# A new order for the opening: w_ada transposed, two tiles projected block by block

## What is computed

```python
c_act = jax.nn.silu(c)
mod = c_act @ w_ada[layer] + b_ada[layer]              # 1024 -> 6 * 1024
shift1, scale1, gate1, shift2, scale2, gate2 = split(mod, 6)
h = rmsnorm(x, norm1_gain[layer]) * (1.0 + scale1) + shift1
proj = h @ w_in[layer]                                 # 1024 -> 1280: q 512 | k, v 256 | p 512
```

## Time and profile before

| | us |
|---|---|
| median of 3 runs | 954.5 (954.21 to 955.22) |
| span of the profiled execution | 952.9 |
| what lies around the span, median less span | 1.6 |
| TensorE busy | 927.6 (97%) |
| VectorE busy | 792.6 (83%) |
| ScalarE busy | 512.9 (54%) |

### The profile page before, as it was taken

How to read it: one execution, slowest core, us unless ns; L and a number is a source line. 1 busy time by engine, 2 the same in 40 slices (tenths; PEclk the granted TensorE clock), 3 DMA queues, 4 the chain that set the end, 5 groups by cost and what they waited for, 6 DMA issues and landing times.

```text
span 952.9 us, 14120 instructions
## 1 busy us (share of the span) xinstructions
PE 927.6 (97%) x4404; PEld 770.8 (81%) x4404; DVE 792.6 (83%) x1205; ACT 512.9 (54%) x980; POOL 276.6 (29%) x243
## 2 busy tenths in 40 slices
PE   4999999999999999999999999999999999999998
PEld 4887888878887777888888888888888888888886
DVE  7979999998689879797787977878798787977797
ACT  3247556676444747456464655546456464655543
POOL 0025554451100100704215070330705215070334
PEclk9999999999999999999999999999999999999999
DMA  9978453348255594655555555745655655555624
GB/s 355 399 236 285 159 197 117 109 156 279 96 155 173 176 340 150 245 206 213 209 187 221 176 185 211 263 140 184 224 215 206 211 191 215 177 188 208 220 88 177
DMA packets 96136, 193.97 MB, mean 204 GB/s; under 512 B 6513, under 2 KB 57441, under 8 KB 96097
## 3 DMA queue, kind: packets, MB, share of 16 engines
q1 hardware_dynamic: 90720, 182.02, 54.2%
q10 hardware_dynamic: 5376, 11.47, 3.5%
HBM read 176.30 MB, written 17.17 MB: 203 GB/s over the span
## 4 chain that ended last, share of the span: by engine, by line
PE 87%; DVE 5%; DMA 4%; ACT 2%; issue 1%; SPq 1%; POOL 0%; ACTq 0%; DVEq 0%; POOLq 0%
PE ps L2117 27%; PE ps L2119 27%; PE ps L2118 27%; DMA bs<-bs_scratch 2%; PE ps L2337 2%; DMA raw_u<-in_w_up 1%; PE ps L2216 1%; DVE acc L1360 1%; PE ps L2363 1%; PE ps L2227 1%; DMA ada_in_raw<-in_w_ada 1%; PE ps L2290 0%; DMA bs_scratch<-stg 0%; DMA m_raw<-mixed_scratch 0%; ACT qbd L832 0%
## 5 line engine op out<-in xcount | busy, mean ns | idle before, releaser
L1283 POOL TENSOR_TENSOR x<-x,p1s 128x512 f32<-128x512 f32 x80 | 116.0, 1470 | 422.0 <-ACT p1s L980 421.3
L2117 PE MATMUL ps<-bs,ring 128*128 128x512 f32 x344 | 134.4, 391 | 1.5 <-DVE h_lo L1724 0.7
L2119 PE MATMUL ps<-bs,ring 128*128 128x512 f32 x344 | 133.9, 389 | 0.0
L2118 PE MATMUL ps<-bs,ring 128*128 128x512 f32 x344 | 133.9, 389 | 0.0
L1731 DVE TENSOR_TENSOR ring<-s,ring 128x512 fp32r<-128x512 f32 x88 | 69.8, 811 | 50.3 <-ACT ring L901 50.2
L2117 PE MATMUL ps<-h_hi,ring 128*128 128x512 f32 x272 | 106.1, 390 | 0.5 <-DVE h_lo L1724 0.5
L2118 PE MATMUL ps<-h_lo,ring 128*128 128x512 f32 x272 | 105.8, 389 | 0.0
L2119 PE MATMUL ps<-h_hi,ring 128*128 128x512 f32 x272 | 105.8, 389 | 0.0
L901 ACT ACTIVATE ring<-s 128x512 fp32r<-128x512 f32 x88 | 53.8, 623 | 66.5 <-PE ps L2119 66.5
L2117 PEld LDWEIGHTS ps<-bs,ring 128*128 128x128 f32 x344 | 64.6, 188 | 16.9 <-DMA bs<-bs_scratch 1.9
L2119 PEld LDWEIGHTS ps<-bs,ring 128*128 128x128 f32 x344 | 64.6, 188 | 13.5
(11 more groups left out here) (291 smaller groups left out, 2333.9 us busy)
## 6 DMA issues: line engine op xcount, KB each, us to landing
bs<-bs_scratch SPq DMA_DIRECT2D x166, 512.0 KB, 6.2
stage<-in_w_ada SPq DMA_DIRECT2D x24, 512.0 KB, 5.9
raw_g<-in_w_gate SPq DMA_DIRECT2D x11, 1024.0 KB, 5.2
raw_u<-in_w_up SPq DMA_DIRECT2D x11, 1024.0 KB, 7.4
raw_d<-in_w_down SPq DMA_DIRECT2D x20, 512.0 KB, 4.1
ada_in_raw<-in_w_ada SPq DMA_DIRECT2D x16, 512.0 KB, 12.4
wi_raw<-in_w_in SPq DMA_DIRECT2D x8, 640.0 KB, 15.3
wo_raw<-in_w_out SPq DMA_DIRECT2D x8, 512.0 KB, 5.7
```

The lines of the kernel that those rows point to most:

```text
L1283: pool.tensor_tensor(x1_half(t, 1), x1_half(t, 1), p1s[j][:, :], ALU.add).then_inc(pool_evac, 1)
L2117: pe.matmul(dst, s_hi, m_hi, start=start, stop=False, skip_group_check=onto)
L2118: pe.matmul(dst, s_hi, m_lo, start=False, stop=False, skip_group_check=onto)
L2119: return pe.matmul(dst, s_lo, m_hi, start=False, stop=stop, skip_group_check=onto)
```

## The change

w_ada is also given transposed by the host. A piece is then 128 outputs by all 1024 inputs, and one multiply with c spread over the partitions (`crow`), with an accumulator output, gives the 128 finished sums as a column (`column_sum`). No reduction on TensorE is left for scale1, shift1, scale2 and shift2; gate1 keeps its own. x tiles 0 and 1 are scaled, split and projected block by block. SP loads w_ada pieces and W_in rows in turns, the shift pieces behind all W_in rows. The shift product comes behind both tiles, only two parts of tile 1 after it. The small vectors, the bias table's store and the constants' loads move between the blocks. `sh_hi` and `sh_lo` lie in the place of tiles that are used later (`s_sb`, `win_a` and `win_b`). Tile 2 of xt goes to `sq_m`.

The core of the diff:

```diff
+            sp.dma_start(vrow[0:KT, :], c[0].rearrange("(r p) -> r p", p=P)).then_inc(c_in, 16)
             sp.dma_start(ident[:, :], identity).then_inc(c_in, 16)
-            sp.dma_start(vrow[0:KT, :], c[0].rearrange("(r p) -> r p", p=P)).then_inc(c_in, 16)
-            def load_first(v, mm, k):
-                sp.dma_start(first_view(v, k), wa_d[k * P:(k + 1) * P, mm * D:(mm + 1) * D]).then_inc(ada_in[k], 16)
+            def load_scale(j):
+                sp.dma_start(first_view(j), wat_d[SCALE1 * D + j * P:SCALE1 * D + (j + 1) * P, :]).then_inc(ada_in[j], 16)
+            def load_shift(j):
+                sp.wait_ge(a1_done, j + 1)
+                sp.dma_start(first_view(j), wat_d[SHIFT1 * D + j * P:SHIFT1 * D + (j + 1) * P, :]).then_inc(ada_in[j], 16)
+            def load_wi(j):
+                sp.dma_start(wi_raw[:, j, :], win_d[j * P:(j + 1) * P, :]).then_inc(piece_in[j], 16)
             def load_xt(t):
-                sp.dma_start(xs[:, t % 2], xt[t]).then_inc(xt_in[t % 2], 16)
-            for k in range(KT):
-                load_first(0, SCALE1, k)
+                sp.dma_start(xs_of(t), xt[t]).then_inc(xt2_in if t == 2 else xt_in[t % 2], 16)
+            load_scale(0)
             load_xt(0)
+            load_wi(0)
+            load_xt(1)
+            sp.dma_start(onehot_sb, onehot).then_inc(table_in, 16)
+            sp.dma_start(table_sb, rel_bias_table).then_inc(table_in, 16)
+            for j in range(1, KT):
+                load_scale(j)
+                load_wi(j)
             for j in range(KT):
-                sp.dma_start(wi_raw[:, j, :], win_d[j * P:(j + 1) * P, :]).then_inc(piece_in[j], 16)
-            load_xt(1)
-            sp.wait_ge(acc1_done, 2)
-            for k in range(KT):
-                load_first(1, SHIFT1, k)
-            sp.dma_start(x_st[:, :], x_d[0:P, :]).then_inc(x_in, 16)
-            sp.wait_ge(hlo_done, 1)
+                load_shift(j)
+                if j == 4:
+                    sp.dma_start(x_st[:, :], x_d[0:P, :]).then_inc(x_in, 16)
+            sp.wait_ge(rel_done, 1)
             load_xt(2)
-            sp.wait_ge(hlo_done, 2)
-            load_xt(3)
             sp.dma_start(g1bc[:, :], b_ada[0, GATE1 * D:(GATE1 + 1) * D].partition_broadcast(P)).then_inc(gate_in, 16)
             sp.dma_start(g2bc[:, :], b_ada[0, GATE2 * D:(GATE2 + 1) * D].partition_broadcast(P)).then_inc(gate_in, 16)
-            sp.wait_ge(mod_done, 2)
+            sp.wait_ge(hlo_done, KT + 1)
+            load_xt(3)
+            sp.wait_ge(shift_sum, KT)
             for n, (mm, k) in enumerate(pieces):
                 if n >= RING:
                     sp.wait_ge(ada_used, n - RING + 1)
-                sp.dma_start(piece_view(n), wa_d[k * P:(k + 1) * P, mm * D:(mm + 1) * D]).then_inc(stage_in[n % RING], 16)
+                src = wa_d[k * P:(k + 1) * P, mm * D:(mm + 1) * D] if mm == GATE1 else wat_d[mm * D + k * P:mm * D + (k + 1) * P, :]
+                sp.dma_start(piece_view(n), src).then_inc(stage_in[n % RING], 16)
                 if (mm, k) == (GATE1, KT - 1):
-                    sp.wait_ge(shift_ps, 3)
                     for j in range(KT // 2):
                         sp.dma_start(wo_raw[:, j, :], wout_d[j * P:(j + 1) * P, :]).then_inc(wo_in[0], 16)
             for j in range(KT // 2, KT):
...
+            def small_vectors():
+                act.wait_ge(small_ps, 4)
+                act.activation(vcol[:, N2:QG], bank(7)[:, N2:QG], ACT.Copy)
...
+                act.activation(vcol[:, QG:QG + 1], bank(7)[:, QG:QG + 1], ACT.Copy, scale=HD ** -0.5).then_inc(vcol_done, 1)
+                act.wait_ge(small_ps, 5)
+                act.activation(rel_sb, bank(6)[0:NQ, 0:3 * CHUNK], ACT.Copy).then_inc(rel_done, 1)
+                act.wait_ge(rel_done, 1)
+                act.dma_start(rel_dram, rel_sb.unsqueeze(1).broadcast_to([NQ, CHUNK, 3 * CHUNK])).then_inc(rel_out, 16)
+            def constants():
+                act.wait_ge(rel_out, 16)
+                for h in range(2):
+                    act.dma_start(bias[h * CHUNK:(h + 1) * CHUNK, 0],
+                                  bass.AP(rel_dram.tensor, h * CHUNK * 3 * CHUNK + CHUNK - 1,
+                                          [[3 * CHUNK - 1, CHUNK], [2 * CHUNK * 3 * CHUNK, NPR], [1, P]])).then_inc(bias_in, 16)
...
+            def h_high_block(j, t0, t1):
+                if j == 0:
+                    xt_landed(act, t0)
+                act.wait_ge(a1_done, j + 1)
+                act.activation(ht_hi[:, t0:t1, j, :], xs[:, t0:t1, j, :], ACT.Copy, scale=a1[:, j:j + 1]).then_inc(hhi_done, 1)
+            def shift_high(j):
+                act.wait_ge(shift_sum, j + 1)
+                act.activation(sh_hi[:, j, :], mod_sum[:, 1, j:j + 1].broadcast_to([P, P]), ACT.Identity,
+                               bias=vcol[:, BA + SHIFT1 * KT + j:BA + SHIFT1 * KT + j + 1]).then_inc(shhi_done, 1)
...
+            wi_high(0, slice(0, QW))
+            h_high_block(0, 0, 1)
+            act.activation(crow[:, :], ps[:, 0:2, :].rearrange("p a b -> p (a b)"), ACT.Copy).then_inc(crow_done, 1)
+            wi_high(0, slice(QW, IN))
+            h_high_block(0, 1, 2)
+            for j in range(1, KT):
+                h_high_block(j, 0, 2)
                 wi_high(j)
-            act.wait_ge(rel_done, 1)
-            act.dma_start(rel_dram, rel_sb.unsqueeze(1).broadcast_to([NQ, CHUNK, 3 * CHUNK])).then_inc(rel_out, 16)
...
+                if j == 2:
+                    small_vectors()
+                if j == 4:
+                    constants()
...
+            for j in range(KT):
+                shift_high(j)
+                if j == 5:
+                    square_x(0)
...
+            def column_sum(piece, row, v, j):
+                return dve.scalar_tensor_tensor(out=piece, in0=piece, scalar=1.0, in1=row, op0=ALU.mult, op1=ALU.mult,
+                                                accum_out=mod_sum[:, v, j:j + 1])
...
+                if mm != GATE1:
+                    ins = column_sum(piece_view(n), crow[:, :], {SCALE2: 2, SHIFT2: 3}[mm], k)
...
+            def scale_column(j):
+                dve.wait_ge(ada_in[j], 16)
+                if j == 0:
+                    dve.wait_ge(small_ps, 3)
+                elif j == 1:
+                    dve.wait_ge(crow_done, 1)
+                row = ps[:, 0:2, :].rearrange("p a b -> p (a b)") if j == 0 else crow[:, :]
+                link(column_sum(first_view(j), row, 0, j))
+                dve.tensor_scalar(a1[:, j:j + 1], mod_sum[:, 0, j:j + 1], b1[:, j:j + 1], vcol[:, N1 + j:N1 + j + 1],
+                                  ALU.add, ALU.mult).then_inc(a1_done, 1)
+            def shift_column(j):
+                dve.wait_ge(ada_in[j], 32)
+                column_sum(first_view(j), crow[:, :], 1, j).then_inc(shift_sum, 1)
...
+            def h_low_block(j, t0, t1):
+                dve.wait_ge(hhi_done, blocks_ready(j, t1 - 1))
+                dve.scalar_tensor_tensor(out=ht_lo[:, t0:t1, j, :], in0=xs[:, t0:t1, j, :], scalar=a1[:, j:j + 1],
+                                         in1=ht_hi[:, t0:t1, j, :].bitcast(F32), op0=ALU.mult, op1=ALU.subtract
+                                         ).then_inc(hlo_done, 1)
+            def shift_low(j):
+                dve.wait_ge(shhi_done, j + 1)
+                dve.scalar_tensor_tensor(out=sh_lo[:, j, :], in0=mod_sum[:, 1, j:j + 1].broadcast_to([P, P]),
+                                         scalar=vcol[:, BA + SHIFT1 * KT + j:BA + SHIFT1 * KT + j + 1],
+                                         in1=sh_hi[:, j, :].bitcast(F32), op0=ALU.add, op1=ALU.subtract).then_inc(shlo_done, 1)
...
+            dve.wait_ge(vcol_done, 1)
+            link(dve.tensor_scalar(b1[:, :], vcol[:, BA + SCALE1 * KT:BA + (SCALE1 + 1) * KT], 1.0, None, ALU.add))
+            scale_column(0)
+            wi_low(0, slice(0, QW), 0)
+            h_low_block(0, 0, 1)
+            wi_low(0, slice(QW, IN))
+            h_low_block(0, 1, 2)
+            for j in range(1, KT):
+                scale_column(j)
+                h_low_block(j, 0, 2)
                 wi_low(j)
-            scale_x(1)
-            h_low(1)
-            fold_first(1)
-            take_first(1, (5, 6))
-            shift_low(0)
-            shift_low(1)
+            for j in range(KT):
+                shift_column(j)
+                if j:
+                    shift_low(j - 1)
             scale_x(2)
-            h_low(2)
+            shift_low(KT - 1)
...
@@ -1610,6 +1631,8 @@
                         last = dve.tensor_copy(dst, v[h].unsqueeze(2).broadcast_to([n, NKV, 2, HD]))
                     last.then_inc(v_done, 1)
                 if it == 0:
+                    scale_x(3)
+                    fold(0)
                     h_low(3)
                     fold(1)
...
+            pe.wait_ge(vrow_in, 16 * 2)
+            pe.transpose(bank(7)[:, 0:N2], vrow[0:N2, :], ident[0:N2, 0:N2]).then_inc(small_ps, 1)
+            pe.wait_ge(cact_done, 1)
```

(74 more changed lines are left out.)

294 lines of the change are left out of this document (89 added, 205 removed).

## The result

The changed kernel takes 973.65 us (median of 4, 972.20 to 973.92) against 954.64 (median of 4, 954.21 to 955.22) for the kernel before. The ratio is 1.0196, 95% interval 1.0181 to 1.0210. The forecast was 966.1 us, range 957.0 to 969.5: right direction and right main mechanism (the stall), but 7.6 us too low, outside the range.

What follows compares the result with a forecast made beforehand. The opening was taken as unhidden, VectorE's chain then TensorE's, with VectorE's arrival counting for the loop. +2.7 opening, +0.8 accumulators, +11.1 stall, -3.0 loop made +11.6 on 952.9: 964.5, as median 966.1 us, range 957.0 to 969.5.

Steps and rivals of the forecast that it cites:

- the stall: ScalarE behind block 4 waits for rel_out, then issues seven DMAs, holding h_high_block(5) until 43.25: +11.1 us.
- The trip: Bias table's store on ScalarE's queue, from end of issue to passed wait: 14.98 us, rel_out at 37.8.
- A: ScalarE's wait behind block 4: rel_out in time, issues don't hold ScalarE, no stall; 955.0 us, chance 0.12.
- B: ScalarE's wait behind block 4: short round trip, but issues still cost 2.3 us; 957.3 us, chance 0.11.
- C: Opening blocks: no stall and a cheaper column sum, ring 4.0 us; 949.9 us, chance 0.04.
- The ring: Opening blocks 1 to 7: column sum, a1, h_high, wi_high, wi_low follow in a loop, 4.55 us a block.
- From evac_q(0) to the first bias add: Stretch ahead of the attention scores: work moves in, about 1.5 us of idle out; 17.2 us against 16.83.
- Rival D: Blocks 5 and 6: TensorE's idle drops its clock to 1.2 GHz, shift product about 5 us late; 971, chance 0.07.
- Attention loop: Two TensorE column reductions of 1.68 us each go from the chain: -3.0 us, bounds 1.5 and 3.4 won.
- Its own sign of being wrong: Attention loop: the forecast is wrong if iterations that held the reductions are no shorter.
- Nothing after the loop: From the last output row of attention to the end: 0 us change forecast.

Runs made afterwards that it cites:

- section 6: Pipelined kernel with the small vectors' copies, constants' loads and table wait moved off the ring: 955.65 us; with 20 filler products ahead of the qT transposes: 955.46.
- section 5: Changed kernel, constants' loads late: wi_high ahead of h_high_block, 960.54 us; instead column sum one block ahead, 963.70; the latter with 30 filler products, 962.51.
- section 3: Attention-loop test: kernel before with TensorE's column reductions each cut from 8 matmuls to 1, 956.42 us; its traces are compared with other kernels'.
- sums cut: Kernel before, with each of the attention loop's two TensorE column reductions cut from 8 matmuls to 1: 956.42 us, ratio 1.0011.
- after, filler: Changed kernel plus 30 products of the matrix of ones on TensorE ahead of the first qT transposes: 973.06 us.
- late, pipelined, filler: Changed kernel with constants' loads late, column sum one block ahead and 30 filler products ahead of the first qT transposes: 962.51 us.
- loads freed: Pipelined kernel with small vectors' copies behind block 4, constants' loads behind the blocks, table wait at shift part 6: 955.65 us.
- loads late: Changed kernel with the rel_out wait and the seven constants' loads moved from block 4 to behind blocks 5, 6 and 7: 963.09 us.
- shift by rows: On loads freed: shift product's q and kv made row by row, pool part last, tile 3 scaled ahead of the first evacuation: 955.38 us.
- SP held: Changed kernel with SP waiting for rel_out before it loads the shift pieces: 969.61 us, one run.

## Why the prediction was wrong, by its steps

**The stall: right.** 11.1 forecast; 10.4 in the trace, 10.6 by taking it out. The trip (14.98 forecast, 15.4) and the time of h_high_block(5) (43.25, 43.80) came as worked out from the earlier trace rows. Rivals A, B and C fell with it.

**The ring: right, its end to 0.3 us in part by luck.** First useful matmul 9.92 (10.2); period 4.68 (4.55 plus 0.1 for the accumulator; its row now says 0.08). evac_q(0) at 71.73, where the steps give 59.55 + 0.8 + 11.1 = 71.45. Three misses of the steps cancel in it: block 1 started 0.4 us early (11.98 against 12.4), the stall was 0.7 shorter (issues of 4.4 us, not 5.4), and block 3 came 1.1 later, for the small vectors' product, which the sum had as free.

**"From evac_q(0) to the first bias add": mis-sized.** 17.2 forecast, 19.1 measured. The prediction had VectorE's idle time moving out of this stretch. But TensorE now gets a gap of 5.3 us ahead of the first transposes, the clock falls, kT and the scores are made at the lower level and VectorE waits 1.46 us for them (0.43 before). About 1.0 us of the 1.9 is the clock (1.1 came back with the filler in section 6, 1.0 in section 5). The rest is idle time that was to move out and stayed: VectorE's waits in this stretch are 2.20 us in sum before and 2.79 after, of which the scores are 1.46, where the prediction took 1.5 off. That makes 2.1 too much waiting; VectorE's own work was 0.2 below its forecast.

**Rival D: right mechanism, wrong place.** I gave it 0.07 on the ground of the earlier trace rows, 1.00 over an opening with 0.67 us of busy time in 10. The clock did fall to 0.50 behind the stall. There it cost next to nothing: VectorE was out of block 7 at 56.28, where the ring and the stall put it at 56.15, and evac_q(0) followed 15.4 us behind (15.3 forecast), so by then TensorE had caught up. It cost at three other places: about 1.1 us at the small vectors in the opening, 1.0 at the transposes and 1.1 in the loop. These 3.2 us are an estimate, added up from the rows above. The rule of the Trainium skill ("TensorE: Matmul & The Clock Gate", Part 1) agrees with the trace: behind both long idle stretches of the opening the clock is at the half level. Shorter stretches, 2.0 to 3.5 us, went either way over the kernels (listed at the end). The first 10 us of the kernel before were no evidence against it, since a clock shown as 1.00 over a start says little. In the changed kernel, under a shown 1.00, the first transposes take 0.42 us each (0.22 apart), as the ones at 85.12 do at the half level (those at 70.08 before took 0.27):

```profile
4.19 1.97 PE L2162 MATMUL ps<-ident,cact 128*128 128x128 f32 x8 [0.61 <-DVE cact L1373]
```

**"Attention loop": the step that failed.** -3.0 forecast, with bounds of -1.5 and -3.4 that left out zero; +1.0 measured, and section 3 got no gain from the reductions alone. The step took the reductions' time on TensorE, 1.68 us each, as won, and found support in the difference of two iterations, 23.00 and 21.16. But those rows have VectorE at 22.19 and 20.29 busy: it filled the longer iteration just as well. The step even used VectorE's 20.3 of 21.16 as its reason to charge the added sums in full, and didn't ask whether an engine so full lets TensorE's time be won at all. Its own sign of being wrong came half true: the iteration of 20.34 us that held a reduction before (131.50 to 151.84) takes 20.66 without it, and the other, of 23.77 us, takes 22.99 (23.77 with the sums cut). The measured +1.0 is +2.0 in the W_out iteration, +1.1 for the clock behind the 3.5 us wait, and -2.1 over the rest (section 3).

**Nothing after the loop: wrong by 1.4.** ScalarE's wait for the load of W_up grew by 2.5 us. SP took longer to issue the eight stores ahead of it (kernel before, then after):

```profile
329.17 6.17 SPq L547 DMA_DIRECT2D bs_scratch<-bs  x8
```
```profile
346.90 7.25 SPq L576 DMA_DIRECT2D bs_scratch<-bs  x8
```

The four stores behind them take 3.60 us to issue instead of 2.78. Every variant of the changed kernel has 7.2 us or more for the eight (7.59 and 7.79 in after, filler and in late, pipelined, filler), the kernel before 6.17 and, with the sums cut, 5.68. The instructions are the same in both programs. Why they are issued slower stays open.

Added up: 2.2 + 4.0 + 1.4 = 7.6 us, the whole miss.

## What to carry to other kernels

- Price a wait by when its data comes, not by where it stands. Each time the ring here got faster, a wait that had been free was reached before its data. List the waits of every engine that the faster part drives, with the time at which each is met.
- When TensorE and VectorE are both 95% busy in a loop, taking work off one may win nothing, as here, unless the other has slack; put zero inside the bounds.
- An idle stretch of TensorE is paid at what stands right behind it only if someone waits there. Look for the short chain of small matmuls behind the gap, and for a small product queued behind the big ones that another engine waits for; a long run of big ones often catches up.

## What the runs showed of the hardware

- The granted clock fell to the 1.2 GHz level behind idle stretches of 2.0, 2.3, 3.5, 5.3 and 11.4 us, but not every time: it stayed at 1.00 behind 2.37 us (loads freed) and behind 3.5 us (loads late, shift by rows). The gap of about 5 us ahead of the transposes brought it down in every trace without filler there, and in none of the three with filler.
- Where VectorE's W_out instructions and GpSimd's window sums ran at the same time, both were slower (5 instructions 8.05 us instead of 6.02; 4 sums 6.60 instead of 3.14). Seen in all these traces, tested apart in none.
- An fp32 product of the 128x128 ones takes two passes of TensorE, 0.23 us in sum (30 in 6.86 us).
- A column sum on VectorE (multiply of 128x1024 fp32 with an accumulator output) takes 1.22 us, and reading the accumulator another 0.08.
- A store of 0.39 MB in 520 packets on ScalarE's queue took 15.4 us beside SP's backlog, and 11.2 with the shift pieces held back. With SP's queue dry it still moved only 197 packets in 2 us.
- Seven small loads block ScalarE for 4.4 us if issued in a row (5.4 in the kernel before, 5.7 with SP held). Put one or two behind each block, they were hidden.
